# Interleaving the two halves of the array in the small matmuls of a two-layer S5 and pooling trunk

## What is computed

```
hn = rmsnorm(x); u_a, u_b = split(hn @ w_in)              # 512 + 512 channels
S5 mixer on u_a: 32 groups of 16 channels, each with a 64-dim complex diagonal state
    bu = B_bar u;  h_t = lam_bar h_(t-1) + bu_t;  y = Re(C h) + D u
    y_a = gelu(y) * sigmoid(gelu(y) @ w_glu)
pooling mixer on u_b: trailing windows 2, 4, 8, 16, then a linear map per group -> y_b
x += [y_a | y_b] @ w_out
x += square(relu(rmsnorm(x) @ w_ff1)) @ w_ff2
```

## Time and profile before

| | |
|---|---|
| median of 3 runs | 2297.27 us |
| profiled execution | 2298.94 us |
| its span | 2297.1 us |
| PE busy | 2158.7 us (94%) |
| PEld busy | 2098.3 us (91%) |
| DVE busy | 1120.3 us (49%) |
| ACT busy | 423.4 us (18%) |
| mean granted clock of TensorE | 0.969 |

### The profile page before, as it was taken

One profiled execution on the slowest core, in us unless ns is written; L12 is line 12 of the kernel. 1 busy time (PEld: TensorE's weight loads), 2 busy tenths in 40 slices (PEclk: granted clock), 3 DMA queues, 4 the chain that ended last, 5 costly groups with the idle time before them and its releaser, 6 DMA issues. The chain is left out here.

```text
span 2297.1 us, 29009 instructions
## 1 busy us (share of the span) xinstructions
PE 2158.7 (94%) x12894; PEld 2098.3 (91%) x12894; DVE 1120.3 (49%) x1622; ACT 423.4 (18%) x483; POOL 120.3 (5%) x80
## 2 busy tenths in 40 slices
PE   4796999999999999999999989999999999999995
PEld 3785889899999999999999878999999999999995
DVE  8885545836354353433356832553433334333344
ACT  3121043201111111111131203421111111111111
POOL 4000003000000000000030000110000000000002
PEclk8898899999999999999999979999999999999997
DMA  3316421112111211221134363111111111111111
GB/s 142 114 57 100 138 64 58 38 38 103 39 65 39 65 56 48 96 72 47 38 115 130 82 137 86 38 46 47 47 37 46 47 47 46 38 47 47 46 37 78
DMA packets 72060, 152.63 MB, mean 66 GB/s; under 512 B 7392, under 2 KB 32512, under 8 KB 71296
## 3 DMA queue, kind: packets, MB, share of 16 engines
q1 hardware_dynamic: 56240, 123.25, 18.3%
q10 hardware_dynamic: 12960, 17.96, 2.5%
q0 software_dynamic: 2736, 9.57, 1.2%
HBM read 123.23 MB, written 27.53 MB: 66 GB/s over the span
## 5 line engine op out<-in xcount | busy, mean ns | idle before, releaser
L1210 DVE TENSOR_TENSOR x<-tile,x 128x816 f32<-128x816 f32 x320 | 216.5, 718 | 563.3 <-PE tile L427 534.1
L427 PE MATMUL tile<-h_high,w_high 128*128 128x408 f32 (+1 forms) x1920 | 430.3, 332 | 44.6 <-DVE h_low L875 36.7
L427 PE MATMUL tile<-h_low,w_high 128*128 128x408 f32 (+1 forms) x1920 | 425.2, 330 | 0.0
L427 PE MATMUL tile<-h_high,w_low 128*128 128x408 f32 (+1 forms) x1920 | 424.2, 329 | 0.0
L427 PEld LDWEIGHTS tile<-h_high,w_high 128*128 128x128 f32 x1920 | 322.6, 190 | 52.2 <-DVE h_low L875 27.4
L427 PE MATMUL tile<-hidden_high,w_high 128*128 128x408 f32 (+1 forms) x1536 | 341.5, 331 | 10.5 <-DVE x L1210 5.4
L427 PE MATMUL tile<-hidden_low,w_high 128*128 128x408 f32 (+1 forms) x1536 | 339.2, 329 | 0.0
L427 PE MATMUL tile<-hidden_high,w_low 128*128 128x408 f32 (+1 forms) x1536 | 338.7, 329 | 0.0
L645 ACT ACTIVATE w_high<-w_raw 128x1024 fp32r<-128x1024 f32 x164 | 172.4, 1051 | 830.8 <-PE tile L427 816.0
L427 PEld LDWEIGHTS tile<-h_low,w_high 128*128 128x128 f32 x1920 | 322.5, 190 | 1.1
L427 PEld LDWEIGHTS tile<-h_high,w_low 128*128 128x128 f32 x1920 | 321.8, 189 | 1.1
(11 more groups left out here) (158 smaller groups left out, 1572.5 us busy)
## 6 DMA issues: line engine op xcount, KB each, us to landing
w_raw<-w_blocks SPq DMA_DIRECT2D x164, 512.0 KB, 3.6
x<-x_t ACTq DMA_DIRECT2D x8, 544.0 KB, 12.6
u_blocks<-ua_dram SPq DMA_DIRECT2D x64, 68.0 KB, 2.8
x<-x_t SPq DMA_DIRECT2D x8, 544.0 KB, 13.4
ya_dram<-u_blocks ACTq DMA_DIRECT2D x64, 68.0 KB, 2.2
y_a<-ya_dram SPq DMA_DIRECT2D x8, 544.0 KB, 3.6
x_kept<-x ACTq DMA_DIRECT2D x8, 544.0 KB, 2.7
x<-x_kept SPq DMA_DIRECT2D x8, 544.0 KB, 13.3
```

The costliest lines, as they stand in the source:

```text
L427: mm = pe.matmul(ps[tile][:, c, 0:(b - a) * J], lhs, xt[:, k, a * J:b * J], start=(first and n == 0), stop=(last and n == 2))
L1210: ins = v.tensor_tensor(xt, pt_, xt, ALU.add)
```

## The change

The matmuls of `kernels`, `drives` and `carry` are the same in number and size; their order on TensorE is another. In `kernels` the half `gl` is now the innermost loop, and both banks are waited for first. In `drives` the loops over halves and parts change places. In `carry` two u's are taken together: first the `kin` matmuls of bank 0 and of bank 1, each behind its wait, and then the eight `cy` matmuls, half and bank in turn. In a bank only the first matmul has `start` set.

```
@@ kernels
-                for gl in range(2):
-                    out = small_at(SM["kernel", l, q, gl])
-                    rows = slice(ST * gl, ST * gl + ST)
-                    for g in range(4):
-                        for ri, b in enumerate((d.bbr, d.bbi)):
-                            mm = pe.matmul(out[0:CH, g * P:(g + 1) * P], b[rows, 4 * q + g, :],
+                outs = [small_at(SM["kernel", l, q, gl]) for gl in range(2)]
+                for g in range(4):
+                    for ri, b in enumerate((d.bbr, d.bbi)):
+                        for gl in range(2):
+                            rows = slice(ST * gl, ST * gl + ST)
+                            mm = pe.matmul(outs[gl][0:CH, g * P:(g + 1) * P], b[rows, 4 * q + g, :],
                                            d.yq[rows, ri, g, 0:BLK, :].rearrange("p t c -> p (t c)"),
                                            start=(ri == 0), stop=(ri == 1))
-                    mm.then_inc(small_done, 1)
+                            if g == 3 and ri == 1:
+                                mm.then_inc(small_done, 1)
@@ drives
-                    for gl in range(2):
-                        for ri in range(2):
+                    for ri in range(2):
+                        for gl in range(2):
@@ carry
-                    for u in range(4 * q, 4 * q + 4):
-                        if u >= 2:
-                            pe.wait_ge(carry_free, l * GP + u - 1)
-                        gl = u % 2
-                        rows = slice(ST * gl, ST * gl + ST)
+                    for u in range(4 * q, 4 * q + 4, 2):
+                        for gl in range(2):
+                            if u:
+                                pe.wait_ge(carry_free, l * GP + u + gl - 1)
+                            for i in range(2):
+                                pe.matmul(sm[gl][:, i * J:(i + 1) * J], kin[:, 2 * (u + i) + gl, :],
+                                          ublk[:, 2 * (u + i) + gl, :], start=(i == 0), stop=False)
                         for i in range(2):
-                            g = u - gl + i
-                            out = sm[gl][:, i * J:(i + 1) * J]
-                            pe.matmul(out, kin[:, 2 * g + gl, :], ublk[:, 2 * g + gl, :], start=True, stop=False)
-                            pe.matmul(out, cy[rows, g, 0, :], w[rows, g, 0, 0:J], start=False, stop=False)
-                            mm = pe.matmul(out, cy[rows, g, 1, :], w[rows, g, 1, 0:J], start=False, stop=True)
-                        mm.then_inc(carry_done, 1)
+                            for ri in range(2):
+                                for gl in range(2):
+                                    rows = slice(ST * gl, ST * gl + ST)
+                                    mm = pe.matmul(sm[gl][:, i * J:(i + 1) * J], cy[rows, u + i, ri, :],
+                                                   w[rows, u + i, ri, 0:J], start=False, stop=(i == 1 and ri == 1))
+                                    if i == 1 and ri == 1:
+                                        mm.then_inc(carry_done, 1)
```

## The result

The changed kernel took 2255.9 us (median of four runs, 2253.69 to 2257.22) against 2295.24 for the kernel before in the same comparison; the ratio is 0.983, with a 95% interval of 0.981 to 0.985. That is 39.3 us less. The forecast was 2257.5, with 40.4 us less on the profiled execution. The profiled executions lie farther apart than the medians: 2253.69 us is the fastest run of the changed kernel and 2298.94 is close to the slowest of the kernel before (2299.1), and their spans differ by 45.2 us.

A forecast was written before the change was run, and what follows sets the result against it. PE, busy 94% of the span, was taken as the bound. Savings of 18.2 + 6.6 + 8.5 + 5.3 + 1.8 = 40.4 us off the profiled 2298.94, adjusted to the median, gave 2257.5 us; range 2250 to 2273.

The forecast's parts named there:

- The wait of the w_glu product: PE's 2.81 us wait for VectorE's z_low stays, since the chain behind the last carry moves with it.
- Carries at full clock: Five calls fall from 8.60 to 4.95 us through fewer row changes and overlapping halves, less a new wait: 18.2 us saved.
- The first case of the rivals: Weight loads of two halves don't overlap in cy, so each pass takes its own slot: 2271.5 us; chance 18%.
- Program order: Drives gain nothing, as their halves already overlap; under strict program order they would gain some 7 us in layer 1.
- Carry(0) of layer 1: At 1.2 GHz throughout, the call takes 9.0 us instead of 15.60: 6.6 us saved.
- the forecast's own range: 2251 to 2266 us, from the clock in layer 0 and carry(0) of layer 1, and some tenths for each wait.
- The first carries of layer 0: Carry(0), carry(1) and wob(4) get shorter from 28.36 us, with a short low-clock stretch assumed: 8.5 us saved.
- the new pause of 2.2 us: Before the fourth pair in layer 0, behind ScalarE's DMA issues; a stretch at 0.50 of about 3.4 us follows, costing 1.7.
- Kernels: Calls take 1.84 us instead of 3.17; the four in the feed-forward part save 5.3 us.
- Kernels in layer 0: The first two calls each keep 0.92 us after a later start, and 1.8 us come through; third and fourth count nothing.

The follow-up runs named there:

- kin_first_only: The kernel before, with the two kin matmuls of each u ahead of its four cy, halves, banks and waits unchanged: 2283.89 us, ratio 0.9952.
- split_only: The changed kernel, with the second pair of u's of six carries inside the next wob tile, behind its first quarter: 2250.15 us, ratio 0.9798 to the kernel before.
- cy_by_half: The changed kernel, with the eight cy matmuls of a pair of u's ordered by half instead of alternating: 2265.39 us, ratio 0.9866 to the kernel before.
- drives_only: The kernel before with only the drives of the change: 2294.78 us in a single run, beside a median of 2296.64 for the kernel before.
- carry_only: The kernel before with only the carry of the change: 2261.7 us, ratio 0.985.
- kernels_only: The kernel before with only the kernels of the change: 2288.31 us, ratio 0.9966.

## Why the prediction was right, point by point

**The bound.** PE's shorter stretches in the carries and in the feed-forward part came through at full length. The wait of the w_glu product stayed at 2.81 us in both layers, as forecast, because the chain behind the last carry moved with it.

**Carries at full clock: 18.2 us forecast, 18.2 measured.** 8.60 to 4.96 us, five times. Its three terms were tried apart: 0.195 us for a change of rows (kin_first_only halved the changes), the pause of 0.55 us, 0.48 of it idle (split_only took it away), and the overlap (cy_by_half took part of it away). It was to be 0.76 us from the last pass's start to the next pair; the starts of single passes in the trace are 0.75 apart.

**The first case of the rivals.** Weight loads of 128 columns to two halves go on at the same time; L570 runs at 0.117 us for a pair, not for a pass. So the 18% for serial loads were spent on a case that the seam of the kernels could not exclude. (Its price was added up too low: 0.94 us for each of 14 pairs and 1.87 for each of two are 16.8, not 15, so that rival stood at 2273.3 us and not at 2271.5.) The Trainium skill (TensorE: Matmul & The Clock Gate, Step-by-step: what each phase is for) gives row tiling no extra bus for weights. It counts buses, and does not say that loads of row tiles must wait for each other. This case's trace shows no such wait at this size: 16 passes with their loads take 1.13 us to the next matmul.

**Program order.** That the drives would gain nothing was read from the earlier trace rows against the Trainium skill (the same page, Part 3, The mechanism), which has matmuls start strictly in program order. drives_only bears the reading out: 0.05 us for a call. And cy_by_half shows both that it happens, in the start at 273.103 us, and its limit, four of eight passes. The measurements decide here: matmuls of different halves do pass each other, over a short distance.

**Carry(0) of layer 1: 6.6 forecast, 8.0 measured, and 1.6 more in the tile behind it.** The sum took 1.2 GHz for the whole call; the clock rose in its second pair. This was in the forecast's own range as 3 us less. The term was too small by these 3 us, and carry_only and split_only, where the clock rose as early, show that it was no single draw. At 1.2 GHz itself the sum held: the first pair takes 4.75 us with its pause of 0.48, where 4.27 and 0.5 were counted.

**The first carries of layer 0: 8.5 forecast, 10.0 measured** (28.36 to 18.32 us). At full clock the order itself brings 5.4 us: 23.75 us in kernels_only, where the old order kept the clock, against 18.32. The other 4.6 are the low stretch that the profile before had drawn. I had given the new pause of 2.2 us a stretch at 1.2 GHz; PE did pause for 2.12 us and no stretch followed in this execution. In two other profiles in which these carries stand at the same place one did:

```profile
261.67 2.18 PE L563 MATMUL small<-u_blocks,intra_weights 128*128 128x136 f32 x8 [3.50 <-ACT u_blocks L773]
```

```profile
250.27:265.53 15.26, 10.70 (x98) 9.36 (x96) 15.07 (x37) 3.11 (x7) 0.00 (x0) 0.89 0.22 38
```

Both are of carry_only: ScalarE's eight DMA issues took 5.13 us there instead of 3.75, the pause was 3.50 us, and the clock fell at 261.7 for 3.4 us. In split_only the pause was 2.54 us and the fall came at 259.9, for 3.4 us. The piece took 21.33 and 20.30 us in these two. The means of three profiles each, 26.3 us with the old order and 20.0 with the new, differ by 6.3 us: half a stretch was a fair mean for the new order, but for the old one the sum had taken the 5.2 us of one profile whole. So the term was some 2 us too large, and that 10.0 were measured is luck of the two executions.

**Kernels: 5.3 forecast in the feed-forward part, 5.3 measured** (four calls from 3.17 to 1.85). The piece as a whole shrank by 5.7, and by 4.8 between the means of four profiles each (before, carry_only, kin_first_only and drives_only against after, kernels_only, cy_by_half and split_only); single ones lie up to 4.3 apart with the same kernels calls.

**Kernels in layer 0: 1.8 forecast, 0.45 in these two profiles.** The rows, to set against the earlier trace rows:

```profile
130.06 0.40 PE L477 MATMUL small<-y_quarter,bbar_re 64*16 64x128 f32 x4 [0.89 <-ACT bt_stage L687]
...
150.74 0.76 DVE L865 TENSOR_TENSOR prep_products<-power_re,prep_in 128x576 f32<-128x576 f32 x1 [1.90 <-PE small L477]
...
231.79 0.68 PE L427 MATMUL tile<-y_b_high,w_high 128*128 128x408 f32 x1 [19.36 <-DVE x L1214]
```

The pause before the first kernel grew from 0.40 to 0.89 us as said, and VectorE's wait fell from 3.54 to 1.90. VectorE goes on at 150.74 instead of 151.81; as this execution was 0.6 us late by then for other reasons (its first drives start at 109.65 instead of 109.06), 1.6 us had really been won there. But then PE, done earlier with its tiles, waits longer for the pooling, 5.69 us instead of 3.93, and the clock is at 1.2 GHz for the sums that follow. Before and after, the windows there:

```profile
194.10:197.40 3.30, 3.30 (x9) 2.09 (x9) 1.18 (x2) 0.00 (x0) 0.00 (x0) 0.50 0.00 0
```

```profile
191.60:198.10 6.50, 5.68 (x14) 3.99 (x15) 2.15 (x4) 1.10 (x2) 0.00 (x0) 0.50 0.00 0
```

The stretch at 0.50 is about twice as long as before (6.5 us of it shown against 3.3), and the pooling sums on VectorE's path run in it: VectorE's three waits there are 2.54, 4.94 and 1.51 us instead of 2.96, 4.30 and 0.92, 0.8 us more in all, and so the first load of intra_weights is issued only 0.3 us earlier (206.32 against 206.61). But the kernels calls are not the only way to such a stretch. The profiles whose code is the same up to the first carry, but for the kernels and drives:

| kernels calls | PE's pause before the pooling sums | at 1.2 GHz behind it | first load of intra_weights issued | start to first carry |
|---|---|---|---|---|
| as before: before | 3.93 | 3.4 | 206.61 | 247.17 |
| kin_first_only | 4.01 | 3.4 | 206.96 | 249.36 |
| carry_only | 4.22 | 6.8 | 208.04 | 250.27 |
| drives_only | 4.22 | 6.8 | 207.88 | 248.71 |
| changed: after | 5.69 | 6.8 | 206.32 | 246.72 |
| kernels_only | 5.44 | 6.8 | 205.74 | 246.01 |
| cy_by_half | 5.54 | 10.2 | 206.31 | 248.05 |
| split_only | 5.47 | 17.1 | 207.63 | 248.34 |

Where the stretch is 6.8 us in both, carry_only and drives_only against after and kernels_only, the first load of intra_weights is issued 1.9 us earlier with the new kernels. Between the means of four, the first carry starts 1.6 us earlier, while profiles of the same calls lie up to 3.1 us apart, about half of it from how long the loads take from there until the first x has landed (23.7 to 25.8 us in the eight). So 0.45 is one draw, and the forecast of 1.8 is not refuted by it. Whether the longer pause makes the longer stretch was not tried by an edit and stays open: all profiles of the table with the longer pause have 6.8 us or more, but so have two with a pause of 4.22, and one and the same code drew 6.8 us in one and 17.1 in another (after, split_only).

**The sum.** 18.2 + 9.6 + 10.0 + 5.3 + 0.45 is 43.6 of the 45.2 us between the two spans. Medians differ by 39.3 us, 34.9 to 44.8 by the interval of the ratio. With the means of the profiles in place of the two single ones (10.2 for carry(0) of layer 1 and its tile, 6.3 for the first carries of layer 0, 1.6 for the start) the same sum is 41.6, an estimate from two to four profiles on each side. So the forecast of 40.4 met the medians with the right mechanism in its largest terms, the carries at full clock and the kernels, and with luck in its clock terms: the one for carry(0) of layer 1 was 3 us too small and the one for the first carries of layer 0 about 2 us too large, and they nearly cancelled. The last step was a slip of half a microsecond: 2298.94 less 40.4 less 1.7 is 2256.8 and not 2257.5.

## What to carry to other kernels

Before interleaving small matmuls over two halves of the array, look at the seams of the old order: groups with twice the count in the same step show whether halves overlap already, and over how many passes. Group matmuls by the number of rows first, since each change between 128 and 64 rows costs (0.195 us here), and alternate halves every one or two matmuls within a group. Before a small gain or loss is read from two profiles, compare the same piece in profiles where it was not touched: here such pieces differed by 2 to 5 us. When two banks then end together, put a piece of a large product between the pairs, so that PE does not wait for the copy.

## What the runs showed of the hardware

- A change between matmuls of 128 rows and of 64 rows costs 0.195 us at 2.4 GHz and 0.30 at 1.2 GHz (kin_first_only, eight changes fewer: 1.56 and 2.38 us).
- Two halves of the array's rows work at once, at 0.110 us for a pair of passes with 128 columns moved and weight loads of 16 columns, and at 0.117 with 136 columns moved and loads of 128.
- TensorE starts work of the other half beside about the last four passes written before it, ahead of three of them. With eight of one half written ahead of eight of the other, 16 passes took 1.70 us to the next matmul instead of 1.13, and four of them overlapped.
- The same order of carries in layer 0 lost the clock near 262 us in the kernel before and not in kernels_only, so that a single profile can hold 4.6 us of such luck.
- In carry(0) of layer 1 the clock rose 3.9 to 6.0 us behind the first matmul with the halves alternating (three profiles), and 19.2 to 21.1 us with the old order (three profiles).
- Eight DMA issues of ScalarE took 3.75 us in the changed kernel and 5.13 in carry_only, and PE's pause behind them was 2.12 and 3.50 us.
